# Gate and up of a SwiGLU stage: one 512-column matmul per weight block for both token halves, halves added by VectorE

## What is computed

```python
def _swiglu(h, w_gate_up, w_down):
    g, u = jnp.split(h @ w_gate_up, 2, axis=-1)
    return (jax.nn.silu(g) * u) @ w_down

for layer in range(DEPTH_2):        # 2 layers
    x = x + 0.5 * _swiglu(_rmsnorm(x, ffn1_norm[layer]), ffn1_w_gate_up[layer], ffn1_w_down[layer])
    x = x + _hybrid_mixer(_rmsnorm(x, mix_norm[layer]), ...)
    x = x + 0.5 * _swiglu(_rmsnorm(x, ffn2_norm[layer]), ffn2_w_gate_up[layer], ffn2_w_down[layer])
```

## Time and profile before

| | |
|---|---|
| Runs of the kernel | 1726.07 us median of 3 (1723.73 to 1726.7) |
| Span of the profiled execution | 1725.0 us |
| TensorE busy (matmul) | 1584.3 us, 92%, 14712 instructions |
| VectorE busy | 871.9 us, 51% |
| ScalarE busy | 633.3 us, 37% |
| GpSimd busy | 248.9 us, 14% |
| DMA | 435.40 MB, mean 252 GB/s |
| Mean granted TensorE clock | 0.972 of full speed |

### The profile page before, as it was taken

The page is one execution under the profiler, slowest core; times in us unless marked ns, Lnnn a source line. Parts: engine busy times, 40 slices in busy tenths (PEclk is TensorE's granted clock), DMA queues, the critical chain, the costliest instruction groups (busy, mean ns, idle before and its releaser), DMA issues.

```text
span 1725.0 us, 34905 instructions
## 1 busy us (share of the span) xinstructions
PE 1584.3 (92%) x14712; PEld 1401.4 (81%) x14713; DVE 871.9 (51%) x1463; ACT 633.3 (37%) x914; POOL 248.9 (14%) x215
## 2 busy tenths in 40 slices
PE   8999997776776677999999999999999999999998
PEld 8889974443333344999999999999999999999998
DVE  5765741111111112865568466556755577475554
ACT  6454421110000001543355553334533355553332
POOL 1120030000000000111115411111111107311110
PEclk9999989999889989999999999999999999999998
DMA  8444599999999999355557445545455566344551
GB/s 344 173 147 147 230 388 428 428 429 429 429 428 429 429 429 425 149 187 189 187 224 252 176 147 184 184 184 206 161 184 184 184 245 250 143 157 184 184 184 62
DMA packets 42562, 435.40 MB, mean 252 GB/s; under 512 B 5067, under 2 KB 5195, under 8 KB 7764
## 3 DMA queue, kind: packets, MB, share of 16 engines
q1 hardware_dynamic: 41716, 429.56, 63.3%
q0 software_dynamic: 736, 4.22, 0.7%
HBM read 430.59 MB, written 3.16 MB: 251 GB/s over the span
## 4 chain that ended last, share of the span: by engine, by line
PE 76%; DMA 14%; DVE 4%; SPq 3%; issue 1%; ACT 1%; POOL 0%; ACTq 0%; DVEq 0%
PE bank L659 21%; PE bank L661 20%; PE bank L660 20%; DMA ring<-moe_w_dram 11%; PE bank L1044 3%; SPq L438 3%; DMA area<-moe_w_dram 2%; PE bank L1068 2%; PE bank L995 1%; PE bank L1219 1%; DVE h_lo L1892 1%; PE bank L1238 1%; PE bank L707 1%; DVE lo_last L1900 1%; PE bank L1224 0%
## 5 line engine op out<-in xcount | busy, mean ns | idle before, releaser
L659 PE MATMUL bank<-h_hi,w_hi 128*128 128x256 f32 x1964 | 559.4, 285 | 2.8 <-DVE h_lo L1892 1.8
L660 PE MATMUL bank<-h_lo,w_hi 128*128 128x256 f32 x1792 | 504.1, 281 | 0.0
L659 PEld LDWEIGHTS bank<-h_hi,w_hi 128*128 128x128 f32 x1964 | 369.9, 188 | 9.3 <-issue 4.5
L660 PEld LDWEIGHTS bank<-h_lo,w_hi 128*128 128x128 f32 x1792 | 337.5, 188 | 0.1
L661 PE MATMUL bank<-h_hi,lo_last 128*128 128x256 f32 x1172 | 329.8, 281 | 0.0
L1607 ACT CAST w_hi<-ring 128x2048 fp32r<-128x2048 f32 x120 | 228.0, 1900 | 67.7 <-PE bank L661 55.6
L661 PE MATMUL bank<-h_hi,lo_first 128*128 128x256 f32 x792 | 222.8, 281 | 0.0
L661 PEld LDWEIGHTS bank<-h_hi,lo_last 128*128 128x128 f32 x1172 | 220.6, 188 | 0.0
L660 PE MATMUL bank<-hid_lo,w_hi 128*128 128x256 f32 x704 | 198.1, 281 | 0.0
L659 PE MATMUL bank<-hid_hi,w_hi 128*128 128x256 f32 x704 | 198.1, 281 | 0.0
L571 POOL TENSOR_TENSOR area<-area,stat 128x256 f32<-128x256 f32 x88 | 106.3, 1208 | 621.1 <-ACT area L1659 621.1
(11 more groups left out here) (432 smaller groups left out, 2690.6 us busy)
## 6 DMA issues: line engine op xcount, KB each, us to landing
ring<-layer_w_dram SPq DMA_DIRECT2D x120, 1536.0 KB, 6.4
ring<-moe_w_dram SPq DMA_DIRECT2D x88, 1536.0 KB, 36.8
area<-moe_w_dram SPq DMA_DIRECT2D x40, 1536.0 KB, 36.8
ring<-first_w_dram SPq DMA_DIRECT2D x21, 1536.0 KB, 6.6
bias_copies_dram<-bias_rows_dram POOLq DMA_DIRECT2D x1, 2048.0 KB, 11.6
h_t<-area SPq DMA_DIRECT2D x32, 64.0 KB, 4.2
ring<-first_w_dram SPq DMA_DIRECT2D x3, 512.0 KB, 6.6
x_t<-x_dram SPq DMA_DIRECT2D x1, 1024.0 KB, 5.0
```

Of the source, the lines that this page charges most:

```text
L659: pe.matmul(out_ap, a_hi, b_hi, start=start, stop=False, **flags)
L660: pe.matmul(out_ap, a_hi, b_lo, start=False, stop=False, **flags)
```

## The change

`h_hi` and `h_lo` become the two planes of one tensor `h_split`. A gate or up weight block's high part multiplies both planes in one 512-column matmul that fills a bank of its own: high x high into the left 256 columns, high x low into the right 256. The weight's low part times the high tokens is added to the left half as before. Gate and up of a chunk have a bank each, and two pairs of banks (2, 3 and 0, 1) rotate instead of four banks. The two halves of each bank are added afterwards: ScalarE copies the right halves of both banks to SBUF, VectorE adds the left halves to them (one instruction of 512 elements each), scales gate, and GpSimd scales up instead of the Silu. gate_up(c) waits from c = 2 on for the sum of chunk c-2. In ScalarE's order `hi_b(c+1)` moves ahead of the Silu.

```diff
-             "h_hi": (KB, T), "h_lo": (KB, T), "hid_hi": (3, T), "hid_lo": (3, T)}, 0)
+             "h_split": (2, KB, T), "hid_hi": (3, T), "hid_lo": (3, T)}, 0)
+        h_hi, h_lo = h_split[:, 0], h_split[:, 1]
...
-        gated, hidden = three["ffn"][:, 0:2, :], three["ffn"][:, 2:4, :]
+        gate_pair = three["ffn"].rearrange("p (n s) t -> p n s t", n=2)
...
-        ps = [ctx.enter_context(nc.psum_tensor(f"bank{i}", [P, 512], F32)) for i in range(8)]
+        bank = ctx.enter_context(nc.psum_tensor("bank", [P, 8, 512], F32))
+        ps = [bank[:, i, :] for i in range(8)]
...
-        GATE_BANKS = ((0, 1, 2, 3), MIXED_BANKS)
+        GATE_BANKS = (2, 0)
...
 GpSimd, scaled():
-                    pool.wait_ge(S("silu_done"), n + 1)
-                    sg = gated[:, n % 2, :]
-                    pool.tensor_tensor(sg, sg, stat[:, 3, :], ALU.mult).then_inc(S("silu_scaled"), 1)
+                    pool.wait_ge(S("gate_scaled"), n + 1)
+                    up = gate_pair[:, n % 2, 1, :]
+                    pool.tensor_tensor(up, up, stat[:, 3, :], ALU.mult).then_inc(S("up_scaled"), 1)
...
 TensorE, gate_up():
-                    q, bank = at + c, GATE_BANKS[f][c % 4]
+                    q, first_bank = at + c, GATE_BANKS[c % 2]
                     pe.wait_ge(S("lo_a_ready"), FIRST_SPLIT + q + 1)
-                    if c >= 4:
-                        pe.wait_ge(S("hid_made"), first_chunk + c - 3)
+                    if c >= 2:
+                        pe.wait_ge(S("halves_summed"), first_chunk + c - 1)
...
-                        m = weight_product(half(bank, side), q, (side * KB + k) * P, h_hi[:, k, :], h_lo[:, k, :],
-                                           start=side == k == 0, stop=k == KB - 1, skip_group_check=True)
+                        cols = slice((side * KB + k) * P, (side * KB + k + 1) * P)
+                        pe.matmul(halves(first_bank + side), hi_of(q)[:, cols], h_split[:, :, k, :],
+                                  start=k == 0, stop=False, skip_group_check=True)
+                        m = pe.matmul(half(first_bank + side, 0), lo_of(q)[:, cols], h_hi[:, k, :],
+                                      start=False, stop=k == KB - 1, skip_group_check=True)
...
 ScalarE, swiglu():
-                    n = CHUNKS * (2 * layer + f) + c
+                    n, first_bank = CHUNKS * (2 * layer + f) + c, GATE_BANKS[c % 2]
+                    a_part_used(act, at + c)
+                    if n >= 2:
+                        act.wait_ge(S("hid_made"), n - 1)
+                    act.copy(gate_pair[:, n % 2], bank[:, first_bank:first_bank + 2, T:2 * T])\
+                        .then_inc(S("halves_copied"), 1)
+                    if c < CHUNKS - 1:
+                        hi_b(at + c + 1)
                     act.wait_ge(S("gate_scaled"), n + 1)
-                    sg = gated[:, n % 2, :]
+                    sg = gate_pair[:, n % 2, 0, :]
                     act.activation(sg, sg, ACT.Silu).then_inc(S("silu_done"), 1)
                     if c:
                         hi_a(at + c + 2)
-                    if c < CHUNKS - 1:
-                        hi_b(at + c + 1)
...
 VectorE, swiglu():
-                    dve.wait_ge(S("a_used"), sum(i % LAYER_SLOTS != FFN2_AT - 1 for i in range(at + c + 1)))
-                    sg, hid = gated[:, n % 2, :], hidden[:, n % 2, :]
-                    tt(sg, ps[bank][:, 0:T], stat[:, 3, :], ALU.mult).then_inc(S("gate_scaled"), 1)
+                    dve.wait_ge(S("halves_copied"), n + 1)
+                    both, sg, hid = gate_pair[:, n % 2], gate_pair[:, n % 2, 0, :], gate_pair[:, n % 2, 1, :]
+                    tt(both, bank[:, first_bank:first_bank + 2, 0:T], both, ALU.add).then_inc(S("halves_summed"), 1)
+                    dve.wait_ge(S("halves_summed"), n + 1)
+                    tt(sg, sg, stat[:, 3, :], ALU.mult).then_inc(S("gate_scaled"), 1)
...
                     lo_b(at + c)
-                    dve.wait_ge(S("silu_scaled"), n + 1)
-                    own(tt(hid, sg, ps[bank][:, T:2 * T], ALU.mult))
+                    dve.wait_ge(S("silu_done"), n + 1)
+                    dve.wait_ge(S("up_scaled"), n + 1)
+                    own(tt(hid, sg, hid, ALU.mult))
```

More of the change, by code:

```diff
@@ L234, in program @@
         SPLIT = 2 * (KB + 3) * T
-        area, hi_front, _, lo_front, hi_back, lo_back, _, h_hi, h_lo, hid_hi, hid_lo = overlaid(
+        area, hi_front, _, lo_front, hi_back, lo_back, _, h_split, hid_hi, hid_lo = overlaid(
             "area", [P, AREA], 0,
@@ L515, in _ @@
             pool.wait_ge(S("bias_row_ready"), 1)
-            pool.dma_start(scratch, bias_row).then_inc(S("bias_stored"), 16)
-            pool.wait_ge(S("bias_stored"), 16)
+            pool.dma_start(scratch, bias_row).then_inc(S("bias_moved"), 16)
+            pool.wait_ge(S("bias_moved"), 16)
             rows_of = MB_HEADS * 2 * T
             pool.dma_start(copies, bass.AP(tensor=scratch.tensor, offset=0, ap=[[0, P], [1, rows_of]]))\
-                .then_inc(S("bias_copied"), 16)
-            pool.wait_ge(S("bias_copied"), 16)
+                .then_inc(S("bias_moved"), 16)
+            pool.wait_ge(S("bias_moved"), 2 * 16)
             src = bass.AP(tensor=copies.tensor, offset=P - 1, ap=[[rows_of - 1, P], [2 * T, MB_HEADS], [1, LOCAL]])
-            pool.dma_start(bias, src).then_inc(S("bias_loaded"), 16)
+            pool.dma_start(bias, src).then_inc(S("bias_moved"), 16)
             def attention():
@@ L2042, in band_spread @@
                 turned = ps[4][:, 0:T].rearrange("p (j h d) -> p h j d", j=TT, h=4)[:, :, :, 0:SUB]
-                dve.tensor_copy(band[:].rearrange("p (h j) d -> p h j d", h=4), turned).then_inc(S("band_copied"), 1)
-                dve.wait_ge(S("band_copied"), 1)
+                own(dve.tensor_copy(band[:].rearrange("p (h j) d -> p h j d", h=4), turned))
                 own(tt(wide, over(band[:], SUB, 3), over(mask, 8, 1), ALU.mult))
@@ L2122, in _ @@
             split_lo(7)
-            dve.wait_ge(S("bias_loaded"), 16)
+            dve.wait_ge(S("bias_moved"), 3 * 16)
             scores_in(0)
@@ L2342, in swiglu @@
                 for c in range(CHUNKS):
-                    n, bank = CHUNKS * (2 * layer + f) + c, GATE_BANKS[f][c % 4]
-                    dve.wait_ge(S("a_used"), sum(i % LAYER_SLOTS != FFN2_AT - 1 for i in range(at + c + 1)))
-                    sg, hid = gated[:, n % 2, :], hidden[:, n % 2, :]
-                    tt(sg, ps[bank][:, 0:T], stat[:, 3, :], ALU.mult).then_inc(S("gate_scaled"), 1)
+                    n, first_bank = CHUNKS * (2 * layer + f) + c, GATE_BANKS[c % 2]
+                    dve.wait_ge(S("halves_copied"), n + 1)
[3 more added lines that the diff above has]
+                    tt(sg, sg, stat[:, 3, :], ALU.mult).then_inc(S("gate_scaled"), 1)
                     if f == 0 and c == 4:
```

## The result

The changed kernel takes 1729.22 us (median of 7 runs, 1727.16 to 1731.29) against 1725.48 for the kernel before (7 runs, 1723.62 to 1726.7): ratio 1.0024, 95% interval 1.0013 to 1.0035. (A ratio in this document is always to the kernel before, with this interval in brackets.) Nine more runs on another chip gave 1729.51 against 1724.93, ratio 1.0032 [1.0021, 1.0043]. The forecast was 1699.5, range 1690 to 1714.5, with 0.92 for faster. It was wrong in size and in sign.

The account below looks back on a forecast made before the run. TensorE, busy 92% of the span, was taken to bound the kernel. 1216 blocks saving 23.8 ns each made 28.9 us, less 2.25 at stage starts: 26.7 us less, forecast 1699.5 us, range 1690 to 1714.5.

Parts of the forecast that it names:

- Why 118.5 ns: Gate and up matmuls: the interval is the longer of weight load (118.5 ns) and streaming of the columns.
- The wide matmul: Gate and up blocks: wide matmul 213.2 ns plus narrow 118.5, so 331.7 instead of 355.5 ns, 23.8 less.
- The first bound: Gate and up blocks: every matmul pays a 12 ns hand-over, block 343.6 ns, time 1714; as a rival, chance 0.13.
- my sum: Steady SwiGLU chunks: 1216 blocks at 23.8 ns give 28.9 us, less 2.25 us lost at stage starts: 26.7 us.
- The stage starts: Third gate_up stalls 1.7 us for the sum, fourth waits for `lo_a(3)`: 0.7 us longer at three stages, 2.25 together.
- the overlap of 0.2: VectorE's queue ahead of `lo_a(3)` at stage starts: neighbouring instructions overlap, saving some 0.2 us.
- 0.4 us twice: VectorE's queue ahead of `lo_a(3)` at stage starts: 0.4 us less wait for GpSimd, twice, its Silu falling out.
- 0.15 us of loss: Start of the first SwiGLU stage: the factor is early, so +0.4 us in the chain costs only 0.15.
- stage ends: Last chunk of a stage: `lo_a` ends 1 us later, costing up to 0.3 us, left to the range.
- the slower one: Rival, wide matmul: at 237 ns or more nothing is saved and the stage-start losses remain; 1731, chance 0.05.
- point of decision: Wide matmul in the slower rival: 235.1 ns is where the block's saving only balances the 2.25 us stage-start loss.
- No clock fell at the starts: Rival, stage starts: the stall lowers TensorE's clock, losing about 1.6 us at each of three; 1704, chance 0.06.

Follow-up runs that it names:

- `b_128cols`: The kernel before, with gate and up's matmuls taking only the first 128 of the 256 token columns; 1701.83 us beside 1723.02 for the kernel before.
- `wide32`: The changed kernel, with the 512-column matmul taking only 32 of the block's 128 weight columns; 1722.71 us beside 1723.02 for the kernel before.
- `b_split3`: The kernel before, with only slot 3 split early (high parts after chunk 0's Silu, low parts ahead of chunk 1's product); 1723.95 us, ratio 0.9996.
- `sum_early`: The changed kernel, with chunk 0's copy and add done before the norm's root and reciprocal; 1723.63 us, ratio 0.9997 to the kernel before.
- `dve_scales`: The changed kernel, with VectorE scaling gate and up in one instruction and GpSimd's scaling removed; 1721.75 us, ratio 0.9989 to the kernel before.
- `after_again`: The changed kernel unchanged, run again on another chip as a level for the stage-start runs; 1729.51 us, ratio 1.0032 to the kernel before.
- `start3`: The changed kernel with chunk 0's sum early, VectorE scaling gate and up without GpSimd, and slot 3 split early; 1718.12 us, ratio 0.9965; again 1717.86, 0.996.

## Why the prediction was wrong

**"Why 118.5 ns" is the step that failed.** I took 118.5 for the weight load, because batches with one column are as slow, and because 22 matmuls at the lower clock took 213.2 ns with nothing on top. Both rows are right, the inference was not. `b_128cols` gives the load alone 110.6 ns, less than 118.6, and `wide32`, with a load of 32 columns beside it, still has 116.9 for the narrow matmul. The one-column batches show that a load can need this long, not that it sets the pace where 256 columns stream. And the lower clock slows the columns to 0.833 ns each: what adds some 6 ns and 0.023 ns a column at the full clock need not show there. A row at one clock gave the total at that clock; it could not tell a hidden load from a limit that shows only at the other.

**"The wide matmul": 213.2 ns taken, 230.4 measured.** The block is 350.7 ns. The first bound, a hand-over paid by every matmul (343.6), had the right kind, but gave the whole excess of 12 ns to the matmul; a part of it (half, by the line above) goes with the columns, which two bounds from one width cannot separate. In my sum the measured block makes 1216 x 4.8 ns = 5.8 us instead of 28.9. The downs take back part: a narrow matmul in the changed stage costs 120.0 to 120.3 ns on average, not 118.6, for which I have no cause. (A wide matmul is not needed for it: the last stage of `b_split3` has none.)
The Trainium skill ("TensorE: Matmul & The Clock Gate", Back-to-back issue gap) has a formula that gives 215.8 ns for an isolated matmul of 512 columns (an estimate worked out from it), and about 131 for one in a stream with loads; the trace agrees with neither, with 230.4 beside narrow matmuls and 233 in an unbroken row.

**The stage starts: mechanism right, size off.** The new wait stood where it was expected: the add was due at 1218.95 and TensorE started at 1218.88. The fourth gate_up was put at 1227.6 and came at 1228.62. (The stall of the kernel before is 0.50 us, not 0.62: 1226.25 is the start of the last down's last matmul, and the next was due 0.12 later.) The chain is in VectorE's timeline of the kernel after:

```profile
1218.04 0.69 DVE L2355 TENSOR_TENSOR area<-bank,area 128x512 f32<-128x512 f32 x1 [0.30 <-ACT area L1665]
1218.77 0.42 DVE L2357 TENSOR_TENSOR area<-area,stat 128x256 f32<-128x256 f32 x1
1219.11 1.22 DVE L1918 TENSOR_TENSOR lo_last<-ring,w_hi 128x1024 fp32r<-128x1024 f32 x1
1221.03 0.42 DVE L2363 TENSOR_TENSOR area<-area 128x256 f32<-128x256 f32 x1 [0.70 <-POOL area L573]
...
1226.28 2.28 DVE L1910 TENSOR_TENSOR lo_first<-ring,w_hi 128x2048 fp32r<-128x2048 f32 x1
```

`lo_a(3)` starts at 1226.28, before at 1224.53: +1.75 us, where the text had +0.7. The two adds moved the queue by 0.73 each (put at 0.69), its start by 0.12 (put at 0.3); the overlap of 0.2 did not come. The large error is GpSimd, from whose earlier start I took 0.4 us twice. GpSimd after, start and duration:

```profile
1219.27 1.66 POOL L573 TENSOR_TENSOR area<-area,stat 128x256 f32<-128x256 f32 x1 [8.37 <-DVE area L2357]
```

and in the kernel before:

```profile
1218.88 1.19 POOL L571 TENSOR_TENSOR area<-area,stat 128x256 f32<-128x256 f32 x1 [7.84 <-ACT area L1659]
```

GpSimd now starts 0.16 us after VectorE's `lo_b`, not 0.61, and takes 1.66 us instead of 1.19. In both kernels it ends 0.6 us after that `lo_b` does (1220.93 against 1220.33; 1220.07 against 1219.49). VectorE's product waits 0.70 us for it, before 0.62: nothing gained, 0.08 lost. `sum_early` has two places where VectorE's neighbours are one column wide instead. There the same GpSimd instruction takes 0.74 us, and it is the two tiny VectorE instructions that last 0.78 us together (0.21 in the changed kernel, where GpSimd's instruction lasted until 0.6 us after the `lo_b` behind them, 1.99 us):

```profile
739.10 0.78 DVE L2345 TENSOR_TENSOR lams<-params 64x1 f32<-64x1 f32 x2
739.12 0.74 POOL L573 TENSOR_TENSOR area<-area,stat 128x256 f32<-128x256 f32 x1 [8.32 <-DVE area L2371]
```

So the two engines' instructions take turns here: beside `lo_b`, some 0.6 of GpSimd's own 0.74 us come after VectorE's end (an estimate from these rows). The Trainium skill ("SBUF — State Buffer", Who interferes with whom) says that a VectorE instruction with two inputs in SBUF contends with a GpSimd instruction that reads SBUF, because its second input comes through the shared read interface. The trace agrees (1.66 and 1.19 us beside `lo_b`, 0.74 without it), and `dve_scales`, with GpSimd out of the queue, lost the waits on `lo_a`.

**Two smaller terms.** In the first stage I counted 0.15 us of loss, since the factor is early there; it lost 1.4, as the same chain of adds and GpSimd runs in it. At stage ends I had up to 0.3 us and left it out of the sum; it is 0.49.

**Of the rivals,** the slower one came nearest in time (1731) and had 0.05. Its point of decision was 235.1 ns for the wide matmul, and at 230.4 that was not reached: the sign came from the starts and ends, 8.4 us instead of 2.25. With these, every block had to save 6.9 ns, and it saves 4.8. No clock fell at the starts, and no wait appeared in mid-stage. What failed in the chances was that nearly all of them hung on one reading of one row.

## What to carry to other kernels

Before a forecast of a merged or widened instruction, get its fixed part and its slope from rows of two widths at the same clock; a row at another clock, or one whose other limit has changed, fits several theories. Where an engine is the bound in the middle of a stage, read the starts of stages apart: instructions that are hidden in mid-stage still stand in the first chain, and waits in series have to be removed together. Starting a GpSimd instruction earlier gained nothing here, since a VectorE instruction with two SBUF inputs ran beside it.

## What the runs showed that was not expected

- The line of about 6 ns + 0.44 ns a column at the full clock. bfloat16 read from the same places has a slope of 0.44 too and nearly no fixed part (113.4 and 226.2 ns), with shorter loads. What makes the slope 0.43 to 0.44 instead of 0.417 stays open: it is not the accumulation or the jump, and loads of 32 columns leave it at 0.43 (228.0 beside 116.9). That the numbers lie 4 bytes apart was not varied.
- A matmul costs the same accumulating or not: 230.6 against 230.4 ns.
- The mixers can hold a stretch at the lower clock, whose place and presence change between kernels that have the same mixer. A mixer takes 128.5 us with one and 125.5 without. Single executions can differ by this much with nothing changed in the stages, and medians may carry a part of it: `sum_early`, 5.9 us under `after_again`, gains more than its starts account for (1 us at each of three, 0.1 at the first). That part was not tried by itself.

Busy time by stretch, columns as in the earlier trace rows; of the kernel after

```profile
1485.00:1490.00 5.00, 5.00 (x25) 5.00 (x25) 3.21 (x9) 4.08 (x12) 2.18 (x1) 0.50 0.32 138
```

and of `start3`, whose stages come some 9 us earlier by then: it has the full clock in the whole of this mixer, here with 87 matmuls in 10 us:

```profile
1480.00:1490.00 10.00, 10.00 (x87) 9.08 (x86) 4.58 (x8) 5.33 (x9) 3.69 (x4) 1.00 0.44 159
```
